# Bias sums moved to a middle pair, a split first load, a reordered seam, one product less

## The reference

```python
proj = jnp.matmul(x_all, w_in)                       # 1024 x 3072: q, k, v of two attention groups
oa, ob = block attention, dilated attention          # 8 heads of 64 each; decoding rows also read caches
o_cat = jnp.concatenate([head_rmsnorm(oa, gn_moba), head_rmsnorm(ob, gn_win)], -1)
hx = layer_norm(DN_ALPHA * x_all + jnp.matmul(o_cat, w_out), ln1_g, ln1_b)
logits = jnp.matmul(hx, w_router) + b_router         # 32 experts, the best 4 of each row
comb = the softmax of those four, spread over the 32 experts
for e in range(32):                                  # acc starts at zero
    gu = jnp.matmul(hx, w_gate_up[e]) + b_gate_up[e]
    gate, up = minimum(gu[:, 0::2], 7), clip(gu[:, 1::2], -7, 7)
    y = jnp.matmul(gate * sigmoid(1.702 * gate) * (up + 1), w_down[e]) + b_down[e]
    acc = acc + comb[:, e] * y
hx = layer_norm(DN_ALPHA * hx + acc, ln2_g, ln2_b)
```

## Time and profile before

| | |
|---|---|
| three runs | 1163.85, 1166.18, 1167.03 us |
| median | 1166.18 us |
| the profiled execution | 1164.79 us |
| its span, first to last instruction | 1162.8 us |
| TensorE busy (PE) | 1105.6 us, 95% |
| VectorE (DVE), ScalarE (ACT), GpSimd (POOL) busy | 293.7, 203.9, 30.0 us |
| DMA | 454.23 MB, mean 391 GB/s |

### The profile page before, as it was taken

One profiled execution on the slowest core, in us unless ns is written; L12 is line 12 of the kernel. 1 busy time (PEld: TensorE's weight loads), 2 busy tenths in 40 slices (PEclk: granted clock), 3 DMA queues, 4 the chain that ended last, 5 costly groups with the idle time before them and its releaser, 6 DMA issues.

```text
span 1162.8 us, 14168 instructions
## 1 busy us (share of the span) xinstructions
PE 1105.6 (95%) x5478; PEld 467.7 (40%) x5479; DVE 293.7 (25%) x734; ACT 203.9 (18%) x481; POOL 30.0 (3%) x65
## 2 busy tenths in 40 slices
PE   7999998999999999999999999999999999999996
PEld 5876764433333333333333333333333333333331
DVE  1453756720303021212121212020202030303123
ACT  1332422411111110202020101010101011111111
POOL 0110111000000000000000000000000000000001
PEclk9999999999999999999999999999999999999998
DMA  9958879799999999999999999999999999999992
GB/s 341 348 184 274 284 259 388 293 380 422 424 429 427 428 428 427 429 427 429 427 429 428 429 427 429 428 429 428 430 427 430 427 430 427 430 428 425 405 411 79
DMA packets 62843, 454.23 MB, mean 391 GB/s; under 512 B 6563, under 2 KB 19507, under 8 KB 35540
## 3 DMA queue, kind: packets, MB, share of 16 engines
q1 hardware_dynamic: 60322, 440.97, 91.7%
q0 software_dynamic: 1728, 10.75, 2.5%
q10 hardware_dynamic: 754, 1.98, 0.5%
HBM read 450.14 MB, written 11.93 MB: 397 GB/s over the span
## 4 chain that ended last, share of the span: by engine, by line
PE 69%; DMA 25%; DVE 2%; ACT 2%; SPq 2%; issue 1%
DMA ring<-in_w_gate_up 24%; PE bank L1167 18%; PE bank L1118 18%; PE bank L676 5%; PE bank L995 5%; PE bank L699 5%; PE bank L1272 2%; PE bank L702 2%; PE bank L860 2%; PE bank L1194 2%; PE bank L991 1%; PE bank L1302 1%; PE bank L817 1%; ACT xtok L1382 1%; ACT actT L1382 1%
## 5 line engine op out<-in xcount | busy, mean ns | idle before, releaser
L1118 PE MATMUL bank<-ring,xg 128*64 128x512 f32 x1904 | 419.3, 594 | 25.7 <-DMA ring<-in_w_gate_up 25.7
L1118 PEld LDWEIGHTS bank<-ring,xg 128*64 128x64 f32 x1904 | 141.3, 137 | 295.3 <-issue 295.2
L1167 PE MATMUL bank<-ring,actT 128*64 128x512 f32 x960 | 216.1, 597 | 3.9 <-ACT actT L1382 3.9
L2038 DVE TENSOR_TENSOR acc<-acc,bank 128x512 f32<-128x512 f32 x60 | 41.3, 688 | 496.8 <-PE bank L1194 496.7
L1532 ACT ACTIVATE sig<-gate 128x256 f32<-128x256 f32 x64 | 26.7, 417 | 541.8 <-DVE gate L2020 541.8
L1167 PEld LDWEIGHTS bank<-ring,actT 128*64 128x64 f32 x960 | 66.7, 137 | 120.3 <-issue 114.5
L2020 DVE TENSOR_SCALAR gate<-bank 128x256 f32<-128x256 f32 x64 | 26.8, 419 | 196.7 <-PE bank L1118 177.8
L699 PE MATMUL bank<-xT,wblk 128*128 128x288 f32 x256 | 67.1, 417 | 2.1 <-DMA wblk<-in_w_in 2.1
L1522 ACT ACTIVATE xg<-bank,small 128x128 f32<-128x128 f32 x128 | 48.0, 457 | 96.7 <-PE bank L676 96.7
L995 PE MATMUL bank<-hx,pick 128*128 128x512 f32 x128 | 59.2, 605 | 0.0
L1194 PE MATMUL bank<-ybuf,spread 128*128 128x512 f32 x120 | 58.4, 618 | 0.0
(11 more groups left out here) (256 smaller groups left out, 728.3 us busy)
## 6 DMA issues: line engine op xcount, KB each, us to landing
ring<-in_w_gate_up SPq DMA_DIRECT2D x119, 2048.0 KB, 25.2
ring<-in_w_down SPq DMA_DIRECT2D x63, 2048.0 KB, 26.8
ring<-in_w_gate_up SPq DMA_DIRECT2D x16, 1024.0 KB, 19.2
wblk<-in_w_in SPq DMA_DIRECT2D x12, 1024.0 KB, 8.3
kring<-in_cache_k_moba SPq DMA_DIRECT2D x16, 256.0 KB, 5.8
vring<-in_cache_v_moba SPq DMA_DIRECT2D x16, 256.0 KB, 5.6
out<-in_state_k_win POOLq DMA_DIRECT2D x8, 512.0 KB, 4.3
out<-in_state_v_win POOLq DMA_DIRECT2D x8, 512.0 KB, 5.6
```

What stands on the lines that cost most here:

```text
L1118: ins = nc.tensor.matmul(bank[n][64 * e:64 * e + 64, :], xg[:, k, 64 * e:64 * e + 64], w[e][:, 512 * n:512 * n + 512], start=False, stop=( ...
L1167: ins = nc.tensor.matmul(bank[4 + half][64 * e:64 * e + 64, :], actT[:, j, 64 * e:64 * e + 64], w[e][:, at:at + 512], start=(j == 0), stop ...
L2038: V.tensor_tensor(o, o, new, ALU.add).then_inc(S.added, 1)
```

## The change

- **Start.** The first block of `w_in` comes in two halves (contraction chunks 0 to 3, then 4 to 7), and `project(0)` waits for the second half at its chunk 4. The first half counts on `S.first_in`, which unit 0 of pair 0 therefore waits for at 32. On ScalarE's queue the loads of the normalisation rows and of the rest of the constants move behind its four copies to xT, and the attention table goes ahead of the constants.
- **Seam.** VectorE does `scale_out(1, 4, 2)` at the head of its step 27. TensorE does chunks 4 and 5 of tile 0 ahead of the second half of the decoding rows, then chunks 6 and 7, and turns the first tile after these. VectorE's raw sums of the first tile go ahead of a memset, `select` and `router_consts`. The product of `keep_warm(1)` goes.
- **Biases.** They move from pair 14 to pair 8 (`MIDDLE`) on TensorE, ScalarE and VectorE; the loops over pairs are cut into two around it. `acc_s` starts as ALPHA * hx * ln1_g directly (four VectorE instructions of 32 x 256), so samp_x, its eight matmuls, the clearing of acc_s and one VectorE addition go.
- **Places.** The ring begins at a multiple of 512 bytes. `first` is written `share_at + 4096`, which is where it lay.

```diff
-    first = place("first", [128, 4096], at=cursor[0] - 16384)
+    first = place("first", [128, 4096], at=share_at + 4096)
...
     share_end = cursor[0]
+    cursor[0] += -cursor[0] % 512
     ring_at = cursor[0]
...
+    MIDDLE = PAIRS // 2
...
+            if n == 0:
+                sp.dma_start(wblk[:, 0, 0:4], w_in_v[:, 0:4, c:c + 256]).then_inc(S.first_in, 16)
+                sp.dma_start(wblk[:, 0, 4:8], w_in_v[:, 4:8, c:c + 256]).then_inc(w_landed[0], 16)
+                return
             sp.dma_start(wblk[:, n % 3], w_in_v[:, :, c:c + 256]).then_inc(w_landed[n % 3], 16)
...
+            if slot == 0:
+                pe.wait_ge(S.first_in, 16)
+            elif c == 0:
                 pe.wait_ge(w_landed[b % 3], 16 * (b // 3 + 1))
...
                 if slot == 0:
                     pe.wait_ge((S.xT_even, S.xT_odd)[k % 2], k // 2 + 1)
+                    if k == 4:
+                        pe.wait_ge(w_landed[0], 16)
...
-        def keep_warm(n):
-            for _ in range(n):
-                nc.tensor.matmul(bank[0][:, :], ident, keep[:, 0:512], start=True, stop=True)
-
         pe.wait_ge(wout_in[2], 16)
         pe.wait_ge(wout_in[3], 16)
+        pe.wait_ge(S.outT_ready, 3)
+        for half in range(2):
+            for k in (4, 5):
+                out_product(0, half, k)
         pe.wait_ge(S.outT_scaled, 2)
         for k in range(4, KC):
             ins = out_samples(k)
         ins.then_inc(S.attended, 1)
-        pe.wait_ge(S.outT_ready, 3)
-        for half in range(2):
-            for k in (4, 5):
-                out_product(0, half, k)
-        turn_hx(0, 0)
-        turn_hx(0, 1)
         pe.wait_ge(S.outT_ready, 4)
         for half in range(2):
             for k in (6, 7):
                 ins = out_product(0, half, k)
             ins.then_inc(S.attended, 1)
+        turn_hx(0, 0)
+        turn_hx(0, 1)
         logits_parts(0)
...
         turn_hx(2, 0)
         place_early()
-        keep_warm(1)
         turn_hx(2, 1)
...
         def add_sample_biases():
-            pe.wait_ge(S.sums_scaled, 2)
-            pe.wait_ge(S.bias_added, 2)
+            pe.wait_ge(S.bias_added, 1)
             for q in range(4):
                 r, c = slice(NS * q, NS * q + NS), slice(256 * q, 256 * q + 256)
-                nc.tensor.matmul(bank[0][r, 0:256], ident[0:NS, 0:NS], samp_x[:, c], start=True, stop=True,
-                                 tile_position=(0, NS * q))
...
-                ins = nc.tensor.matmul(bank[1][r, 0:256], combT[:, SEQ:T], bdn[:, c], start=True, stop=True,
+                ins = nc.tensor.matmul(bank[0][r, 0:256], combT[:, SEQ:T], bdn[:, c], start=True, stop=True,
                                        tile_position=(64, NS * q))
...
-        with pe.Fori(1, PAIRS // 2 - 1) as m:
+        with pe.Fori(1, MIDDLE // 2) as m:
+            finish(m * 2, m, 0, m)
+            finish(m * 2 + 1, m, 1, m + 1)
+        finish_with_biases(MIDDLE, MIDDLE // 2, 0, MIDDLE // 2)
+        finish(MIDDLE + 1, MIDDLE // 2, 1, MIDDLE // 2 + 1)
+        with pe.Fori(MIDDLE // 2 + 1, PAIRS // 2 - 1) as m:
             finish(m * 2, m, 0, m)
             finish(m * 2 + 1, m, 1, m + 1)
         last = PAIRS - 1
-        finish_with_biases(last - 1, last // 2, 0)
+        finish(last - 1, last // 2, 0, None)
...
-            pe.wait_ge(S.bias_added, 5)
             begin_gate_up(last)
...
+        for k in range(1, KC, 2):
+            act.wait_ge(S.x_turned, k + 1)
+            copy(xT[:, k, :], bank[k][:, 0:T]).then_inc(S.xT_odd, 1)
         act.dma_start(gn_rows[0:4, :], gn_moba.rearrange("a (k p) -> (a k) p", p=128)).then_inc(S.gn_in, 16)
...
+        act.dma_start(att[:, :], att_table[:, 0:A_END]).then_inc(S.att_in, 16)
         act.dma_start(keep[:, C_TRI:C_END], keep_table[:, C_TRI:C_END]).then_inc(S.consts_in, 16)
...
+            if slot == 27:
+                scale_out(1, 4, 2)
             if slot in MSQ:
                 take_squares(MSQ[slot])
...
                 samp_place(1)
-                scale_out(1, 4, 2)
                 scale_out(2, 6, 2)
...
-            for half in range(2):
-                c = slice(512 * half, 512 * half + 512)
-                V.scalar_tensor_tensor(samp_x[:, c], hx[0:NS, 2, c], ALPHA, ln_g[0:NS, c], ALU.mult,
-                                       ALU.mult).then_inc(S.sums_scaled, 1)
+            for q in range(4):
+                c = slice(256 * q, 256 * q + 256)
+                ins = V.scalar_tensor_tensor(acc_s[NS * q:NS * q + NS, :], hx[0:NS, 2, c], ALPHA, ln_g[0:NS, c], ALU.mult,
+                                             ALU.mult)
+            ins.then_inc(S.added, 1)
...
-            V.memset(acc_s[:, :], 0.0).then_inc(S.added, 1)
...
+        raw_sum(0, 0)
+        raw_sum(0, 1)
         link(V.memset(lg[:, 2, :], 0.0))
         select(0, 0)
         router_consts()
-        raw_sum(0, 0)
-        raw_sum(0, 1)
         moments(0, 0)
...
+        with dve.Fori(0, MIDDLE) as i:
+            next_pair(i)
+        next_pair(MIDDLE, with_biases=True)
+        with dve.Fori(MIDDLE + 1, PAIRS - 2) as i:
+            next_pair(i)
```

More of the change, by code:

```diff
@@ L164, in build_layer @@
     ln_gs, ln_bs = place("ln_gs", [128, 256]), place("ln_bs", [128, 256])
-    late_at = cursor[0]
     parts = spread[:, 0:128]
-    samp_x = place("samp_x", [NS, D])
     bdn = hx[64:64 + E + 1, 2, :]
-    combT = place("combT", [128, T], at=late_at)[64:64 + E + 1, :]
+    combT = place("combT", [128, T])[64:64 + E + 1, :]
     wrt = place("wrt", [128, KC, E], at=share_at)
@@ L226, in build_layer @@
         y_ready mixed added y_varied y_rooted y_scaled y_centred y_gained y_normed y_done y_moments y_shared
-        sums_whole sums_scaled copies_out
+        sums_whole copies_out
         results_out dve_done dve_moe pass_added""".split()
@@ L1107, in gate_up @@
                     w = [first[:, 2048 * e:2048 * e + 2048] for e in range(2)]
-                    pe.wait_ge(S.first_in, 16)
+                    pe.wait_ge(S.first_in, 32)
                 elif whole:
@@ L1220, in finish, with finish_with_biases @@
                              1: lambda: (pe.wait_ge(S.actT_ready, i * 2 + 2), turn_slots(i + 1, 1))}, whole)
-            gate_up(i + 1, m_next, 1 - odd, {3: lambda: combine(i)}, next_whole)
-        def finish_with_biases(i, m, odd):
+            if m_next is not None:
+                gate_up(i + 1, m_next, 1 - odd, {3: lambda: combine(i)}, next_whole)
+        def finish_with_biases(i, m, odd, m_next):
             def first_slots():
@@ L1243, in finish_with_biases @@
             down(i, m, odd, {0: first_slots, 1: other_slots, 2: other_biases}, True)
+            pe.wait_ge(S.bias_added, 5)
+            gate_up(i + 1, m_next, 1 - odd, {3: lambda: combine(i)}, True)
         begin_gate_up(0)
@@ L1386, in _ @@
             copy(xT[:, k, :], bank[k][:, 0:T]).then_inc(S.xT_odd, 1)
+        act.dma_start(gn_rows[0:4, :], gn_moba.rearrange("a (k p) -> (a k) p", p=128)).then_inc(S.gn_in, 16)
+        act.dma_start(gn_rows[4:8, :], gn_win.rearrange("a (k p) -> (a k) p", p=128)).then_inc(S.gn_in, 16)
+        act.dma_start(ln_rows[0:4, :], ln1_g.rearrange("a (k p) -> (a k) p", p=256)).then_inc(S.gn_in, 16)
+        act.dma_start(ln_rows[4:8, :], ln1_b.rearrange("a (k p) -> (a k) p", p=256)).then_inc(S.gn_in, 16)
         act.dma_start(att[:, :], att_table[:, 0:A_END]).then_inc(S.att_in, 16)
+        act.dma_start(keep[:, C_TRI:C_END], keep_table[:, C_TRI:C_END]).then_inc(S.consts_in, 16)
         act.dma_start(blk[:, :], att_table[:, A_END:A_END + 160]).then_inc(S.blk_in, 16)
@@ L1558, in between_pairs, with between_with_biases @@
             take_down(i)
-        def take_comb():
+        def between_with_biases(i):
+            take_gathered(i + 1)
+            take_weights(i)
+            take_turned(i)
             act.wait_ge(S.comb_turned, 1)
             copy(combT[0:E, :], bank[3][0:E, 0:T]).then_inc(S.combT_ready, 1)
-        with act.Fori(0, PAIRS - 2) as i:
+            take_slots(i + 1)
+            take_down(i)
+        with act.Fori(0, MIDDLE) as i:
             between_pairs(i)
             sigmoids(i + 1)
-        take_gathered(PAIRS - 1)
-        take_weights(PAIRS - 2)
-        take_turned(PAIRS - 2)
-        take_comb()
-        take_slots(PAIRS - 1)
-        take_down(PAIRS - 2)
+        between_with_biases(MIDDLE)
+        sigmoids(MIDDLE + 1)
+        with act.Fori(MIDDLE + 1, PAIRS - 2) as i:
+            between_pairs(i)
+            sigmoids(i + 1)
+        between_pairs(PAIRS - 2)
         sigmoids(PAIRS - 1, (0, 1))
@@ L2047, in add_biases @@
             dve.wait_ge(S.bias_sums, 5)
-            link(V.tensor_tensor(acc_s[:, :], acc_s[:, :], bank[0][:, 0:256], ALU.add))
-            V.tensor_tensor(acc_s[:, :], acc_s[:, :], bank[1][:, 0:256], ALU.add).then_inc(S.bias_added, 1)
+            V.tensor_tensor(acc_s[:, :], acc_s[:, :], bank[0][:, 0:256], ALU.add).then_inc(S.bias_added, 1)
         largest_counts()
@@ L2057, in _, with next_pair @@
```

(11 more changed lines are left out.)

8 lines of the change are left out of this document (removed).

## The result

The changed kernel takes 1150.61 us (median of 4 runs, 1149.27 to 1152.87), the kernel before on the same chip 1166.61 (1163.85 to 1167.16). Rival B had named 1152.4.

The account below looks back on a forecast made before the run. DMA was taken as full from 240 us to the tail, the end set by the stream's start, its rate and TensorE's work after the last waits. Start +0.9, seam -3.3, tail -4.3: -6.7, so 1159.5 us; range 1154 to 1163.5.

Parts of the forecast that it names:

- Rival B: Stream of loads: the aligned ring is faster by 0.8%, 7 us more gained, 1152.4 us; chance 0.08.
- start: First w_in products: 1.7 us lost to a low clock after a longer pause, keys 0.8 sooner; net 0.9 us later.
- seam: Before the first gate_up: new order gives 2.35 us, the removed product 0.94; together 3.3 us sooner.
- tail: Last pairs: 5.4 us of bias work leaves TensorE, about 1 becomes a wait for w_down; 4.3 us gained.
- Alignment: Ring's start in SBUF: two windows showed 428 and 426 GB/s, taken as one rate; costed at nothing.
- Rival C: Stream of loads: the aligned ring is slower, rows land at 422 GB/s, 12.5 us lost, 1172 us; chance 0.05.
- Rival A: Start: no low clock after the new pause, 1.7 us better than forecast, 1157.8 us; chance 0.15.
- keys 0.8 us sooner: Start: first cached keys land 0.8 us sooner, as the constants queue on the other side and later.
- The point that the prediction puts at 202.6: Seam: TensorE's end of a copy and the router's parts, after the 32-row tile's turns; 204.97 in the kernel before.
- The product: Seam: the unread product of 128 x 512 stands on the chain; removing it gains 0.94 us.
- Rival D: Seam: gain hidden or eaten by lower clock or late VectorE, about 1 us left; 1162.6 us; chance 0.16.
- Pair 8: Middle: 4.8 us more TensorE work there, covered by 20 us of load slack; costed at nothing.

Follow-up runs that it names:

- e1: The kernel before with only the ring moved to start at a multiple of 512 bytes; ratio to the kernel before 0.9952.
- e3: The kernel before with only the ring moved to start 256 bytes past a multiple of 512; ratio to the kernel before 0.9964.
- e2: The changed kernel without the line that aligns the ring; ratio to the kernel before 0.9945.
- e6: The kernel before with only the start's part of the change, ring unaligned; ratio to the kernel before 1.0003.
- e11: The changed kernel with the biases back in pair 14 and samp_x as before; ratio to the kernel before 0.9908.
- e4: The kernel before with only the biases moved to pair 8 and acc_s made without samp_x; ratio to the kernel before 0.9974.
- e5: The kernel before with only the seam's part of the change, ring unaligned; ratio to the kernel before 0.9954.
- e8: The kernel before with the start's part and the ring at a multiple of 512 bytes; ratio to the kernel before 0.9942.
- e9: The changed kernel without the start's part; ratio to the kernel before 0.9871.
- e7: The changed kernel with the unread product of 128 x 512 put back; ratio to the kernel before 0.9872.

## Why the prediction missed, step by step

Against the second profiled execution of the changed kernel (1149.3 of span; before 1162.8) the account is:

| step | forecast | measured | from |
|---|---|---|---|
| start | +0.9 | -0.5 | w_out 162.71 for 163.18 |
| seam | -3.3 | -3.5 | w_out to gate_up 60.32 for 63.84 |
| stream: alignment, pair 8 | 0 | -5.4 | S 891.82 for 897.25 |
| tail | -4.3 | -4.1 | T 18.53 for 22.67 |
| sum | -6.7 | -13.6 | |

The first profiled execution (1151.0) has -0.4, -3.5, -3.7 and -4.1, in sum -11.8: its load of unit 8 took 23.1 us from issue to landing where that of the second took 20.8, and no run tells why. The medians are 1.8 us further apart than the profiled executions of the table (15.4 for 13.6). A likely part of this is that the kernel before was profiled in an execution that kept full clock at the seam, which four of six with its order did not.

**Alignment was the step that failed**, "I cost alignment at nothing". It gave 6.5 us of stream and another 1.2 us of earlier keys. The two short windows of the earlier trace rows were the wrong rows. One such window can't show 1%: with the ring aligned the stretch at 203 to 207 us reads 424 GB/s, 2 less than unaligned, and 430 in e1 and e3. The better comparison was in front of me: 422 against 428 GB/s, both with rows of 8 KiB, one over 60 us into the ring and one into the aligned `first`. The second is a short window too, so it was a reason to give the rival more, not a proof.

The Trainium skill ("DMA: Bandwidth & Descriptors", How a descriptor splits into AXI transactions) was named in the prediction with about 7 us and set aside. On e1, e2 and e3 the measurement agrees with it, 256 bytes as the unit included. That page of the Trainium skill speaks of bytes that are fetched, while here it is the place that is written which is off; that a start off by 128 bytes costs time there too is what these runs add. An estimate from the beats of 32 bytes that the Trainium skill gives there counts four additional beats for a start 128 bytes past, which is 12.5% of a row of 1 KiB, 1.6% of 8 KiB and 0.8% of 16 KiB. The windows show 7% (374 to 400, with other sizes among them), 1.2% and 0.7%.

Rival B had the mechanism and nearly the size; it should have had the larger chance, since two short windows were all that spoke against it. Rival C is refuted by e1; its mechanism had no ground either, for the eight buffers are 16 KiB each and began at the same place within 512 bytes before.

**The start** had the right mechanism and a wrong size. The pause before the keys (3.0 us, and 4.2 in e2 with its unaligned buffers; forecast some 4), the clock of 0.50 behind it and its price (1.7 us) are as forecast in both profiled executions of the changed kernel. Rival A, full clock after the pause, didn't come true there; e6 and e11 show that it can. The term that failed is "keys 0.8 us sooner" from the queue's order: the order gives nothing in e6 against e4 and e5 (and 0.1 to 0.7 us between the aligned kernels), the alignment 1.2 us (e8 against e6), and the remaining 0.9 is that the kernel before happened to be profiled with its keys late, 22.62 for the 21.7 to 21.8 of e4 to e6. The low clock isn't a fixed price but falls in some executions only. Of the start of a kernel the Trainium skill says something like it ("TensorE: Matmul & The Clock Gate", The HAM clock gate, which calls the number of slow matmuls there run-variable); here pauses in the middle of a kernel show it, by the three values 140.56, 142.25 and 143.37 us above.

**The seam** held. The point that the prediction puts at 202.6 stands at 201.92; from the first product of the samples that is 2.67 us gained instead of 2.35. The product gives 0.86 where 0.94 was forecast. What was missed is the clock: the pauses "that cost nothing" in the earlier trace rows cost 1.5 to 3.0 us in four executions of six. Rival D is wrong as to the changed kernel; its low clock ahead of the gather came in e2 and e9, for 1.7 us.

**The tail** held in size: T changed by -4.1 us where 4.3 was forecast (the prediction's own rows give 4.2), with 1.28 us of waiting for w_down ahead of L1307. In the second profile that wait is gone, and TensorE takes unit 8 at 1114.89, just after it landed at 1114.85: loads and TensorE end together. What the prediction didn't have is that this step and the alignment help each other a little. With the biases still in pair 14, TensorE kept 0.4 and 1.2 us of what the stream gained at full clock (e1, e11), and 2.3 and 2.5 us with a stretch at half clock in that pair (e3, e8).

**Pair 8** was costed at nothing. DMA's rate didn't drop there, but among the aligned kernels S is 890.4 to 890.8 with the biases in pair 14, and 891.3 to 891.9 (once 893.5) with them in pair 8: about 1 us. One difference is on the pages: the queue that fetches instructions moved 34 packets (0.56 MB) in every execution with the biases in pair 8 and 26 (0.43 MB) in every other, which is the code of the cut loops that the prediction left at nothing. At 431 GB/s that is 0.3 us of DMA, an estimate; what the rest is, no run tells. It isn't the stretch at half clock that both profiled executions of the changed kernel and e9 had near 934 us: e7 had none, and its S is the same (891.9 for 891.8 and 891.7).

## What to carry to other kernels

Where DMA is the bound, give every buffer that loads write a start at a multiple of 256 bytes (128 past one is the only other place that was tried here), and test a rate over a long, full stretch and on short rows: a window of 4 us can't tell 1%. An earlier start pays only as far as what the next step waits for comes with it, so move that load first. Two gains of which one frees the loads and the other TensorE should be costed together, since each hides what the other gives.

## What was not expected of the hardware

- 128 bytes off in SBUF cost 7% of the rate in a stretch of short rows (374 for 400 GB/s in e2 and e1), 1.2% at rows of 8 KiB (422 for 427) and 0.7% at 16 KiB (428 for 431).
- A pause of TensorE of 1.2 and then 1.7 us brought 1.2 GHz for 3.4 us in three executions, for 6.8 us in one, and left 2.4 GHz in two, with the same code there. It cost 1.5 to 1.7 us and 3.0. A profile of one execution can miss such a cost.
- A stretch of 3.4 us at half clock cost 1.7 us at 22 us, where TensorE sets the path, and nothing that S shows near 934 us, where the loads do.
